# Norms ahead of split products in a two-pass float32 model kernel: squares by ACT, parts taken straight from the turned rows' PSUM banks

## The reference

```
y = x * rsqrt(mean(x * x, axis=-1) + 1e-6) * gain      # rms_norm, float32
x = x + part(y)                                        # part: a mixer, a swiglu, the experts
swiglu(y) = (silu(y @ wg) * (y @ wu)) @ wd
```

## Time and profile before

| what | value |
|---|---|
| median of three timed runs | 2724.45 us |
| profiled execution, its own time | 2722.08 us |
| its span | 2720.0 us |
| PE busy | 2622.2 us, 96% |
| VectorE busy | 1901.7 us, 70% |
| ACT busy | 1406.0 us, 52% |
| mean granted clock of TensorE | 0.993 |
| HBM | 615.07 MB, 226 GB/s mean |
| chain that ended last | PE 83%, DVE 10%, ACT 3%, DMA 2%, issue 2% |

### The profile page before, as it was taken

The page is one execution under the profiler, slowest core; times in us unless marked ns, Lnnn a source line. Parts: engine busy times, 40 slices in busy tenths (PEclk is TensorE's granted clock), DMA queues, the critical chain, the costliest instruction groups (busy, mean ns, idle before and its releaser), DMA issues.

```text
span 2720.0 us, 46988 instructions
## 1 busy us (share of the span) xinstructions
PE 2622.2 (96%) x18619; PEld 2273.2 (84%) x18619; DVE 1901.7 (70%) x2847; ACT 1406.0 (52%) x2256; POOL 0.2 (0%) x4
## 2 busy tenths in 40 slices
PE   8899999988999999999999999999999999999998
PEld 7675998846999999999999988954999999865897
DVE  3755555747888888888888888774655655664654
ACT  2412333334777777777777777272443443353432
POOL 0000000000000000000000000000000000000000
PEclk9999999998999999999999999999999999999999
DMA  6536442575999899989898988020645552321541
GB/s 261 232 144 251 186 184 77 211 318 207 334 338 339 340 342 336 341 336 342 332 347 327 350 324 319 16 94 11 248 183 186 186 186 94 114 103 70 193 185 55
DMA packets 57000, 615.07 MB, mean 226 GB/s; under 512 B 6448, under 2 KB 6704, under 8 KB 6704
## 3 DMA queue, kind: packets, MB, share of 16 engines
q1 hardware_dynamic: 56448, 610.20, 59.5%
q10 hardware_dynamic: 432, 3.15, 0.3%
HBM read 612.28 MB, written 1.05 MB: 225 GB/s over the span
## 4 chain that ended last, share of the span: by engine, by line
PE 83%; DVE 10%; ACT 3%; DMA 2%; issue 2%; DVEq 0%; SPq 0%; ACTq 0%
PE psum L1677 8%; PE psum L1679 8%; PE psum L1678 8%; PE psum L322 6%; PE psum L324 6%; PE psum L323 6%; PE psum L512 4%; PE psum L1706 4%; PE psum L1708 4%; PE psum L1707 4%; PE psum L337 3%; PE psum L338 3%; PE psum L339 3%; PE psum L664 2%; DMA ring<-stream_dram 2%
## 5 line engine op out<-in xcount | busy, mean ns | idle before, releaser
L406 DVE TENSOR_TENSOR r_high<-ring,r_high 128x1024 fp32r<-128x1024 f32 x936 | 1090.1, 1220 | 115.8 <-ACT r_high L368 115.0
L368 ACT ACTIVATE r_high<-ring 128x1024 fp32r<-128x1024 f32 x624 | 626.3, 1059 | 6.4 <-DMA ring<-stream_dram 6.4
L1677 PE MATMUL psum<-r_high 128*128 128x256 f32 x1792 | 510.9, 285 | 13.0 <-DVE r_high L1903 12.9
L1679 PE MATMUL psum<-r_high 128*128 128x256 f32 x1792 | 507.7, 283 | 0.0
L1678 PE MATMUL psum<-r_high 128*128 128x256 f32 x1792 | 507.4, 283 | 0.0
L322 PE MATMUL psum<-r_low,r_high 128*128 128x256 f32 x1408 | 399.8, 284 | 1.7 <-DVE r_high L482 1.7
L324 PE MATMUL psum<-r_low,r_high 128*128 128x256 f32 x1408 | 398.4, 283 | 0.0
L1677 PEld LDWEIGHTS psum<-r_high 128*128 128x128 f32 x1792 | 341.8, 191 | 37.7 <-DVE r_high L1903 13.4
L1678 PEld LDWEIGHTS psum<-r_high 128*128 128x128 f32 x1792 | 342.0, 191 | 4.4
L1679 PEld LDWEIGHTS psum<-r_high 128*128 128x128 f32 x1792 | 342.3, 191 | 0.0
L372 ACT ACTIVATE r_high<-ring 128x1024 fp32r<-128x1024 f32 x312 | 329.4, 1056 | 0.0
(11 more groups left out here) (509 smaller groups left out, 4224.7 us busy)
## 6 DMA issues: line engine op xcount, KB each, us to landing
ring<-stream_dram SPq DMA_DIRECT2D x384, 1536.0 KB, 8.2
arena<-bias_dram ACTq DMA_DIRECT2D x2, 1024.0 KB, 8.0
pack<-pack_dram SPq DMA_DIRECT2D x1, 1664.0 KB, 16.6
const<-const_dram SPq DMA_DIRECT2D x1, 1060.0 KB, 13.1
x<-x_dram SPq DMA_DIRECT2D x1, 1024.0 KB, 5.1
xc<-ctx_dram SPq DMA_DIRECT2D x1, 1024.0 KB, 24.5
arena<-band_dram ACTq DMA_DIRECT2D x1, 1024.0 KB, 5.1
out_dram<-x SPq DMA_DIRECT2D x1, 1024.0 KB, 3.9
```

Of the source, the lines that this page charges most:

```text
L368: act.activation(w_hi[:, i % 2, part * D:part * D + D], slot_of[r][:, part * D:part * D + D], ACT.Copy)\
L406: ins = dve.tensor_tensor(lo, slot_of[r][:, o:o + D], hi.bitcast(f32), SUB)
L1677: pe.matmul(dst, xe_hi[:, k, :], hi, start=(k == 0), stop=False)
L1679: ins = pe.matmul(dst, xe_lo[:, k, :], hi, start=False, stop=(k == KD - 1))
```

## The change

The squares and the root. Behind each residual add ACT squares a tile as soon as both of its halves are added (`squares_act`, with a root of a constant ahead of them), and takes the root of the sums itself, scale and 1e-6 inside that instruction (`tokens_root_act`). The adds go by halves of 512 columns (`add_half_dve`); the last down products raise a mark per bank (`marks`), and the last tile of `out_tile_pe` is computed half after half.

Norms 1 and 2 no longer use `hT`: ACT writes the high part of each turned chunk directly from its bank, with the gain (`rows_hi_act`), and VectorE the low part from the same bank, bank times gain minus high part (`rows_lo_dve`), after ACT has passed each half. Norms 3 and 7 keep the evictions. The first block's third part is split behind x instead of ahead; at norm 2 the root stands ahead of the pieces, one piece ahead of x and three behind, and TensorE begins with the first half of x. Fillers: 8 to 6 ahead of `e_ffn`, 9 to 4 and 5 to 4 around norm 2, 4 to 3 ahead of norm 3, 5 to 4 ahead of norm 7. The final result is stored in four pieces.

```diff
+        def squares_act(act):
+            act.activation(eps_root, eps_col, ACT.Sqrt)
+            for j in range(NT):
+                roots[0] += 1
+                squares[0] += 1
+                act.wait_ge(sem("rms_in"), roots[0])
+                act.activation(xn[:, j, :], x_tm[:, j, :], ACT.Square, accum_out=ss[:, j:j + 1]).then_inc(sem("x_squares"), 1)
+
+        def tokens_root_act(act, n):
+            act.wait_ge(sem("x_squares"), squares[0])
+            act.activation(inv_rms[:, 0:n], ss[:, 0:n], ACT.Sqrt, scale=1.0 / D, bias=eps_col).then_inc(sem("rms_out"), 1)
...
+        def rows_hi_act(act, k, gain, hi, name):
+            for c in range(KD):
+                if c % 2 == 0:
+                    act.wait_ge(sem("norm_tr"), 4 * k + c // 2 + 1)
+                ins = act.activation(hi[:, c, :], chunk_ps(c), ACT.Copy, scale=gain(c))
+                if c % 4 == 3:
+                    ins.then_inc(sem(name), 1)
+
+        def rows_lo_dve(dve, src, gain, hi, lo, hi_name, hi0, lo_name, filler, rstd_ctx=None):
+            rstd = tokens_root_dve(dve, NT if rstd_ctx is None else 2 * NT)
+            dve.tensor_scalar(rows_tm[:, 0, :], src[:, 0, :], rstd[:, 0:1], None, MUL)
+            step(dve, dve.tensor_scalar(rows_tm[:, 1, :], src[:, 1, :], rstd[:, 1:2], None, MUL), "norm_xn")
+            if rstd_ctx is not None:
+                step(dve, dve.tensor_copy(rstd_ctx, rstd[:, NT:2 * NT]), "dve_step")
+            filler()
+            for half in range(2):
+                dve.wait_ge(sem(hi_name), hi0 + half + 1)
+                for c in range(4 * half, 4 * half + 4):
+                    ins = dve.scalar_tensor_tensor(lo[:, c, :], chunk_ps(c), gain(c), hi[:, c, :].bitcast(f32), MUL, SUB)
+                if half or lo_name == "px_lo":
+                    ins.then_inc(sem(lo_name), 1)
...
         def ffn_dve(dve, q, name, spread=None, meanwhile=None):
-            ffn_x_lo_dve(dve, swiglu, q, 0)
+            split_dve(dve, swiglu, ffn_at(name, q, 0), 0, 2, 3)
             split_dve(dve, swiglu, ffn_at(name, q, 1), 1)
+            if meanwhile:
+                meanwhile()
...
+        def add_tokens(dve, q, dst, scale_row=None, tmp=None, name="rms_in"):
+            for j in range(NT):
+                for hf in range(2):
+                    if 2 * j + hf < 2 * NT - 1:
+                        out_tile_dve(dve)
+                    else:
+                        dve.wait_ge(sem("ffn_dn"), (q + 1) * NB_FFN)
+                    add_half_dve(dve, dst, j, hf, 0, scale_row, tmp, name if hf or name != "rms_in" else "dve_step")
...
         def out_tile_pe(pe, n0, lhs, j, first, last):
+            for hfs in ((0,), (1,)) if last else ((0, 1),):
+                for k in range(KD):
+                    n = n0 + k // 3
+                    if first and k % 3 == 0:
+                        slot_ready(pe, n)
+                    w = slot_of[n % RING]
+                    for hf in hfs:
+                        o = (k % 3) * D + hf * 512
+                        ins = pe.matmul(psum[:, 2 * j + hf, :], lhs(k)[:, j * P:(j + 1) * P], w[:, o:o + 512],
+                                        start=(k == 0), stop=(k == KD - 1))
+                    if last and 1 in hfs and (k % 3 == 2 or k == KD - 1):
+                        ins.then_inc(w_used[n % RING], 1)
+                if 0 in hfs:
+                    ins.then_inc(sem("out_tile"), 1)
...
                 for half in range(2):
+                    if s == 0:
+                        pe.wait_ge(sem("px_lo"), half + 1)
...
         def diff_act(act):
+            first_pieces_act(act, qkv_split, 0, 1)
+            rows_hi_act(act, 2, lambda c: vec("o_ln_mix", c), x_hi, "px_hi")
+            first_pieces_act(act, qkv_split, 1, qkv_split["n"])
...
+            for b in range(2 * NT):
+                sp.wait_ge(sem("x_final"), b + 1)
+                sp.dma_start(out[:, 512 * b:512 * b + 512], x[:, 512 * b:512 * b + 512]).then_inc(sem("stored"), 16)
...
-            idle_pe(pe, 8)
+            idle_pe(pe, 6)
             ffn_pe(pe, 0, "e_ffn")
-            idle_pe(pe, 9)
-            norm_pe(pe, 2)
-            idle_pe(pe, 5)
+            idle_pe(pe, 4)
+            norm_pe(pe, 2, rows_tm)
+            idle_pe(pe, 4)
...
-            root_act(act, 2 * NT)
-            ffn_act(act, 1, 0, "e_ffn")
-            first_pieces_act(act, qkv_split)
-            root_act(act, NT)
+            squares_act(act)
+            tokens_root_act(act, 2 * NT)
+            ffn_act(act, 1, 0, "e_ffn", lambda c: vec("e_ln_ffn", c))
+            squares_act(act)
+            tokens_root_act(act, NT)
             diff_act(act)
```

More of the change, by code:

```diff
@@ L237, in root_act, with norm_dve @@
             act.activation(inv_rms[:, 0:n], mean_sq[:, 0:n], ACT.Sqrt).then_inc(sem("rms_out"), 1)
-        def norm_dve(dve, k, src, gain, shift, off, meanwhile=None, summed=False, xn=xn, rstd_ctx=None, bank=0):
-            for j in range(0 if summed else NT):
+        def norm_dve(dve, k, src, gain, shift, off, meanwhile=None, summed=False, xn=xn, rstd_ctx=None, bank=0, rooted=False):
+            for j in range(0 if summed or rooted else NT):
                 step(dve, dve.tensor_tensor_reduce(xn[:, j, :], src[:, j, :], src[:, j, :], 1.0, 0.0, MUL, ADD,
                                                    ss[:, j:j + 1]), "dve_step")
-            rstd = inverse_root_dve(dve, ss[:, 0:NT if rstd_ctx is None else 2 * NT], D)
+            n = NT if rstd_ctx is None else 2 * NT
+            rstd = tokens_root_dve(dve, n) if rooted else inverse_root_dve(dve, ss[:, 0:n], D)
             if rstd_ctx is not None:
@@ L325, in gate_up_pe, with down_pe @@
             ins.then_inc(sem(s + "_gu"), 1)
-        def down_pe(pe, f, at, i, first, last):
+        def down_pe(pe, f, at, i, first, last, marks=False):
             r, turn, blk = at
@@ L339, in down_pe @@
                     ins = pe.matmul(dst, h_lo, hi, start=False, stop=last)
+                    if marks and 2 * j + hf < 2 * tiles - 1:
+                        ins.then_inc(sem("out_tile"), 1)
             ins.then_inc(sem(s + "_dn"), 1)
@@ L398, in blocks_act, with split_dve @@
                 stage(i)
-        def split_dve(dve, f, at, i):
+        def split_dve(dve, f, at, i, first=0, end=3):
             r, turn, blk = at
-            for part in range(3):
+            for part in range(first, end):
                 o = part * D
@@ L503, in out_tile_pe @@
-        def out_tile_pe(pe, n0, lhs, j, first, last):
[L505 to L517, removed]
+                for hf in range(2):
+                    if 2 * j + hf < 2 * NT - 1:
+                        out_tile_dve(dve)
+                    else:
+                        dve.wait_ge(sem("ffn_dn"), (q + 1) * NB_FFN)
+                    add_half_dve(dve, dst, j, hf, 0, scale_row, tmp, name if hf or name != "rms_in" else "dve_step")
@@ L1282, in piece_dve, with first_pieces_act @@
             dve.tensor_tensor(lo, src, hi.bitcast(f32), SUB).then_inc(sem("piece_lo"), 1)
-        def first_pieces_act(act, f):
-            act.wait_ge(sem("ffn_dn"), f["done"])
-            for i in range(f["n"]):
+        def first_pieces_act(act, f, i0, i1):
+            if i0 == 0:
+                act.wait_ge(sem("ffn_dn"), f["done"])
+            for i in range(i0, i1):
                 piece_act(act, f, i)
```

142 lines of the change are left out of this document (75 added, 67 removed).

## The result

| | before | after |
|---|---|---|
| median of the timed runs | 2726.58 us (4, 2723.17 to 2729.95) | 2706.56 us (4, 2704.89 to 2708.18) |
| profiled execution, its span | 2722.08, 2720.0 | 2708.18, 2706.4 |
| PE / VectorE / ACT busy | 2622.2 / 1901.7 / 1406.0 | 2618.7 / 1889.4 / 1417.8 |
| mean granted clock | 0.993 | 0.991 |

The ratio is 0.9926, 95% interval 0.991 to 0.9942: 20.0 us faster by the medians, where 19.2 were forecast, and 2706.56 where the forecast had 2705. The profiled pair shows only 13.6, since before's profiled execution was one of its fastest and after's its slowest. So the seams are read one by one, from the end of the last product (at A, C and D from VectorE's first add behind it) to the mark named in the table, at A, B and D the first product of the next stage.

The account below looks back on a forecast made before the run. TensorE bounds most of the span, so only seams can gain: 4.1 + 8.4 + 1.7 + 0.8 + 2.4 + 3.2 - 1.4 = 19.2 us, from median 2724.45 to 2705; range 2699 to 2713.

Parts of the forecast that it names:

- A: Seam from output projection to first feed-forward (norm 1): TensorE's fillers set the start, 245.6 instead of 249.7, 4.1 us gained.
- C: Seam from attention to experts (norm 3): one half add left, 2.27 to the reciprocal against 3.03, 0.8 us gained.
- D: Seam from last output projection to last feed-forward (norm 7): half passes and third split part moved, 2.4 us gained.
- B: Seam from first feed-forward to attention's projection (norm 2): start at 446.5 behind fillers instead of 454.9, 8.4 us gained.
- largest item, the pieces: At seam B, weight pieces no longer stand ahead of ACT's root: reciprocal at 439.35 instead of 444.25, 4.9 us.
- B's clock: Behind seam B, fillers up to the first product keep full clock where it was 0.66: 1.7 us more gained.
- E: End of the kernel: half passes bring 1.3 and the smaller last store 1.9, 3.2 us gained.
- F: Reordered last output tile before the paired feed-forward: ring slot freed 4.1 us later, 1.4 us lost (0 to 2.8).
- 1: Rival: fewer fillers let the clock fall at stage starts; gain 14.1 us, 2710.3; chance 0.12.
- 2: Rival: late refills queue up and the pair stage waits; F costs 6 us, gain 14.6, 2709.9; chance 0.09.
- 3: Rival: ACT's square displaces the root's table, two loads at each of four seams; gain 8.8 us, 2715.7; chance 0.03.
- 4: Rival, slower: TensorE held at 1.2 GHz far into the first feed-forward; at 60 us, 2734; chance 0.03.

Follow-up runs that it names:

- the repeat: The changed kernel run again with no edit: 2706.47 us, ratio 0.9926.
- extra router fillers: Changed kernel with fillers ahead of norm 3 back at four and two more behind its 16 transposes: 2705.76 us, ratio 0.9923.
- the whole tile: Changed kernel with the last output tile of the first conditioned layer computed both halves side by side, as before: 2707.85 us, ratio 0.9931.

## Why the prediction was right, step by step

- **What bounds it.** Right. The first feed-forward took 187.3 before and 187.6 after, the last one 188.96 in both; all of the gain lies at seams. That the stretches between only shift did not hold in the profiled pair: the seams gain 18.0 there, and 4.4 are lost again between them (1.6 ahead of A, 1.8 in router and experts, 0.9 in the conditioned layers, 0.1 in feed-forward and attention), most of it with low-clock patches.
- **Common prices.** New subtract 3.2 taken, 3.22 measured. Gain copies 3.9 taken, 3.0 measured, off the path at A. Square to reciprocal 1.55 taken, 1.6 measured.
- **A, 4.1.** Reciprocal unmoved (3.03 both), fillers bind: right. The table's 3.2 sets the low clock after against the full clock before. Like with like it is 4.9 at full clock (16.5 to 11.6) and 4.5 at the low clock (17.8 to 13.3): the profile of the kernel before with the root first has the same seam A as the kernel before, and there the low clock fell too. The forecast missed 0.6 of this by the filler term: it took the fillers' row for the time to the next product, 5.3 for twelve passes, and that product starts 0.6 before the row ends. It also took the clock at A for safe, since the stage behind it had run at 1.00.
- **B, 8.4.** 8.9 measured; 4.8 of it the reciprocal, forecast 4.9. The 0.5 more is the same filler term. The name "largest item, the pieces" holds in the changed kernel (5.4 at the reciprocal and 8.3 at the start lost with the pieces back) and not alone (1.7 in the kernel before): the steps share one chain, so an item's worth depends on which others are in.
- **B's clock, 1.7.** Won at B, as the 1.00 shows; whether it is a gain of the whole is open. Each profile carries low-clock patches elsewhere: summed up to the last product, before's loses 17.1 us to them and after's 22.2 (22.2, 20.5 and 20.5 in the repeat and the profiles with extra router fillers and with the whole tile). A patch at 520 in the attention is there in most profiles after and was not before, at the same 1.7. But before's profiled execution is no average one: its mean clock is 0.993, that of 35 others 0.990, and that of nine of the changed kernel 0.991. By these means the changed kernel loses less to the clock, by some 3 us as an estimate (the clocks are given to three digits). At an equal mean clock of 0.991 the executions lie 18.0 apart (2724.15, nine of them, and 2706.18, three).
- **C, 0.8.** 0.73 at the reciprocal. Two of the profiles lose 1.3 and 1.5 in the router's stretch again (27.9 and 28.1 for before's 26.7), which leaves -0.5 and -0.7, within the bound of -1.
- **D, 2.4.** 2.43, and bound by VectorE.
- **E, 3.2.** 2.7. The adds brought 1.3; of the store I took 2.0 for a quarter, without a row, and it is 2.5. The estimate from the Trainium skill (DMA: Bandwidth & Descriptors, Anatomy of one DMA) was 2.6, and the trace agrees; its 4.4 for the whole is above the 3.9 of the trace. That page fits its figures to transfers issued by GpSimd, and these stores are issued by SyncE.
- **F, -1.4.** The step that failed: about -0.1. Its first half held (refill issued 4.1 later forecast, 4.3 measured; landed 4.0). Then I let the table load follow VectorE's add; it ran at 1905.40, while the wait came only ahead of the SiLU at 1908.90. That takes 1.3 off the chain, more than the 0.9 that the chain itself was to lose; the other 0.5 of the 1.4 stood for refills disturbing each other, of which the intervals show nothing.
- **Sum.** At full clock 4.9 + 8.9 + 0.7 + 2.4 + 2.7 - 0.1 = 19.5, 20.0 by the medians, whose interval is some 4 us to either side. C and D were within 0.1, A, B and E within 0.8. That 19.2 came so close is in part luck: A and B 1.3 too small and F's cost 1.3 too large made up for E's 0.5 and for the clock's 1.7, which this sum leaves out.
- **Rivals.** 1: tested without fillers, real, but not reached by this change. 2: refuted by the whole tile. 3: refuted by the rows of B: the root begins at 437.80, 2.06 behind the last product, which a half add of 0.7, a square of 1.06 and its read-out fill, and the next copy follows at 438.00; there is no room for a load of 1.28 on either side, and ACT's timeline has none between the constant's root at 431.96 and 447.74. 4: refuted, the feed-forward runs at 1.00.

## What to carry to other kernels

Read a seam as one chain across engines and find the last arrival again after each edit: here it went from ACT's pieces to VectorE to TensorE's own fillers, and the same edit was worth 1.7 us alone and 5.4 to 8.3 in company. Filler matmuls have a right count, near the one that ends with the operand; none cost 3 us and before's number 6. Where executions of one kernel lie 3 to 10 us apart, read a microsecond from intervals between marks that repeat to 0.1 us, and only the total from the medians.

## What the runs showed of the hardware that was not expected

- With nearly the same seams, TensorE's granted clock drops to the 1.2 GHz level for short patches at a handful of places (around 82 to 146, 240, 520, 620, 650, 1775, 2375), most of them 1.7 or 3.4 us lost, around the router 5.1 to 8.5. Which of them appear differs between profiles of one instruction sequence: seam A has the patch in three profiles (start 10.25, 10.24 and 10.22 after the reciprocal) and not in three others (8.57 each), and TensorE was doing the same before it in all six. The kernel before shows the same at its seam A (13.48 and 14.75). The Trainium skill (TensorE: Matmul & The Clock Gate, Part 1) says that the monitor behind the clock runs free of the program; the trace agrees in that one sequence is found at either level.
- The quarter store, alone at the end, takes 2.5 us from issue to landing and the whole 3.9: a quarter of the bytes saves 1.4.
